# Clearing a gate table in HBM: 20 of its 32 writes issued one stage earlier

## The reference

```
xn = rmsnorm(x);  qa ka va qb kb vb ga gb = split(xn @ w_in)
oa = stick_breaking_attention(qa, ka, va)      # 8 heads
ob = sliding_window_attention(qb, kb, vb)      # 8 q heads, 2 kv heads, window 128, bias, sinks
x  = x + (sigmoid(ga) * (oa @ w_oa) + sigmoid(gb) * (ob @ w_ob)) @ w_o
# product-key experts on t = rmsnorm(x): 8 heads, the best 16 of 128*128 experts each
s, e = top16(scores of t @ wq with the subkeys);  g = softmax(s)
x  = x + sum over heads and choices of  g * gelu(u[e] . t) * v[e]
y  = rmsnorm(x)
```

## Time and profile before

| | us |
|---|---|
| median of three runs | 3921.8 |
| lowest and highest | 3915.57, 3924.2 |
| the profiled execution, its own time | 3913.63 |
| its span in the trace | 3911.9 |
| `route_sample`, first SP instruction to that of `project` | 311.81 to 392.48 |
| `window`, first SP instruction to that of `decide` | 868.26 to 997.75 |

### The profile page before, as it was taken

One profiled execution on the slowest core, in us unless ns is written; L12 is line 12 of the kernel. 1 busy time (PEld: TensorE's weight loads), 2 busy tenths in 40 slices (PEclk: granted clock), 3 DMA queues, 4 the chain that ended last, 5 costly groups with the idle time before them and its releaser, 6 DMA issues. The chain is left out here.

```text
span 3911.9 us, 44636 instructions
## 1 busy us (share of the span) xinstructions
PE 3533.0 (90%) x14123; PEld 2094.6 (54%) x14147; DVE 2613.2 (67%) x5036; ACT 842.1 (22%) x1599; POOL 1655.6 (42%) x1245
## 2 busy tenths in 40 slices
PE   7998799886789999999925999999999999999998
PEld 6445579885466676776722444444444444444443
DVE  0441777755248543545575888888888878888886
ACT  1451211114333345446200000100001000010001
POOL 0000068740123788888772343333333334333331
PEclk8899899997899999999967999999999999999999
DMA  7793389978688775676939999999999999999994
GB/s 267 313 421 145 112 345 395 383 284 300 234 293 284 187 184 108 138 171 115 209 84 397 389 414 400 399 400 373 407 388 394 398 379 404 381 395 406 389 416 179
DMA packets 424235, 1201.13 MB, mean 307 GB/s; under 512 B 150472, under 2 KB 215416, under 8 KB 345336
## 3 DMA queue, kind: packets, MB, share of 16 engines
q0 software_dynamic: 168496, 680.80, 47.0%
q1 hardware_dynamic: 187600, 505.84, 35.0%
q10 hardware_dynamic: 67968, 12.45, 1.8%
HBM read 1127.33 MB, written 72.68 MB: 307 GB/s over the span
## 5 line engine op out<-in xcount | busy, mean ns | idle before, releaser
L2156 POOL DMA_INDIRECT d_ring<-peer_uv,d_idx x512 | 654.3, 1278 | 1081.5 <-DVEq L2210 975.3
L2313 PE MATMUL d_ps<-d_xd,d_u 128*128 128x512 f32 x2048 | 907.4, 596 | 105.6 <-DMA d_u<-u_blocks 87.9
L2324 PE MATMUL d_ps<-d_v,d_a 128*128 128x512 f32 x2048 | 913.6, 600 | 38.8 <-DVE d_a L2216 32.3
L2208 DVE SCALAR_TENSOR_TENSOR d_acc<-d_ring,d_aw,d_acc 128x1024 f32<-128x1024 f32 x512 | 657.7, 1285 | 98.7 <-DVE d_acc L2208 63.6
L2313 PEld LDWEIGHTS d_ps<-d_xd,d_u 128*128 128x128 f32 x2048 | 391.4, 191 | 601.2 <-issue 589.6
L1544 POOL DMA_INDIRECT G<-c_cellg,c_cell x384 | 633.4, 1649 | 142.8 <-issue 120.0
L2324 PEld LDWEIGHTS d_ps<-d_v,d_a 128*128 128x128 f32 x2048 | 393.5, 193 | 540.0 <-issue 539.9
L2196 DVE SCALAR_TENSOR_TENSOR d_ring<-d_ring,d_xn 128x1024 f32<-128x1024 f32 x512 | 605.5, 1220 | 95.3 <-DMA d_qacc<-ys 51.4
L837 POOL DMA_INDIRECT a_x<-peer_uv,a_rowu x128 | 165.9, 1296 | 544.4 <-DVE k_rowv L907 500.9
L2278 ACT ACTIVATE d_ge<-d_h (+1 forms) x256 | 52.1, 203 | 1168.3 <-DVE d_ring L2196 1168.2
L2002 PE MATMUL c_ps<-c_mT,c_chunk 128*128 128x128 f32 x2048 | 239.6, 277 | 8.6 <-DMA c_chunk<-wq 7.5
(11 more groups left out here) (360 smaller groups left out, 4277.7 us busy)
## 6 DMA issues: line engine op xcount, KB each, us to landing
c_chunk<-wq SPq DMA_DIRECT2D x128, 512.0 KB, 4.9
d_u<-u_blocks SPq DMA_DIRECT2D x128, 512.0 KB, 19.1
d_v<-v_blocks SPq DMA_DIRECT2D x128, 512.0 KB, 16.7
s_kc<-sb_kT SPq DMA_DIRECT2D x32, 1024.0 KB, 9.5
s_vc<-sb_v SPq DMA_DIRECT2D x32, 1024.0 KB, 7.4
c_chunk<-w_m SPq DMA_DIRECT2D x64, 512.0 KB, 5.1
d_gb<-G SPq DMA_DIRECT2D x32, 1024.0 KB, 36.0
G<-b_zeros SPq DMA_DIRECT2D x32, 768.0 KB, 8.2
```

What stands on the lines that cost most here:

```text
L2156: pool.indirect_dma_start(out=ring[:, b], out_offset=None, in_=a["peer_uv"], in_offset=bass.IndirectOffsetOnAxis(ap=idx8[par][:, b:b + 1], ...
L2208: nc.vector.scalar_tensor_tensor(acc[T % 2][:], ring[:, b, D:], aw[:, bass.ds(col + n, 1)], acc[T % 2][:], ALU.mult, ALU.add).then_inc(sum ...
L2313: last = nc.tensor.matmul(ps[:, HB + x % 2, :], ub[j][:, k], xd[:, k].rearrange("p t q -> p (t q)"), start=(k == 0), stop=(k == KC - 1))
L2324: last = nc.tensor.matmul(ps[:, VB + c % 4, :], A[u][j][:, q * P:(q + 1) * P], vb[u][j][:, half * 512:half * 512 + 512], start=(j == 0), s ...
```

## The change

Twenty of the 32 writes, rows 0 to 79 of G, are issued in `route_sample`, by SP behind its loads, from a tile of zeros of its own that GpSimd fills; SP waits for them before the block ends. In `window` the eight writes ahead of the loop are gone, and each of its six turns issues two writes instead of four, rows 80 to 127; the wait at the end is for these twelve.

```diff
+CLEARED = 80
 # route_sample
+        zeros = sb("r_zeros", [P, 4, FIRST_HOT * P])
+        zero_done, zero_st = sem("r_zero_done"), sem("r_zero_st")
 # SP, behind the loads of w_r and wq
+                sp.wait_ge(zero_done, 1)
+                for b in range(0, CLEARED, 4):
+                    sp.dma_start(o["G"][b:b + 4, :, 0:FIRST_HOT * P].rearrange("b p t -> p b t"), zeros[:]).then_inc(zero_st, 16)
+                sp.wait_ge(zero_st, 4 * CLEARED)
 # GpSimd
+                nc.gpsimd.memset(zeros[:], 0.0).then_inc(zero_done, 1)
                 for done in spent:
                     pool.sem_clear(done)
 # window, SP
                 sp.wait_ge(zero_done, 1)
-                clear_gates(0, 8)
                 with sp.Fori(0, NP // 2 - 1) as i:
...
                         load_v(t + 1, 1 - u)
-                        clear_gates(32 + 16 * t, 4)
+                        clear_gates(CLEARED + 8 * t, 2)
                 sp.wait_ge(pe_b.sem, pe_b.at(NP - 3, "values"))
                 load_v(NP - 1, 1)
-                sp.wait_ge(zero_st, 16 * P // 4)
+                sp.wait_ge(zero_st, 4 * (P - CLEARED))
```

## The result

The changed kernel takes 3911.55 us in the median of 20 runs, the kernel before 3925.41 on the same chip in 20. The ratio is 0.9963, interval 0.9952 to 0.9974: faster by 14.5 us (10 to 19). The forecast was 23.0 us. Applied to the 3921.8 us from which I predicted, the ratio gives 3907.3, inside my range of 3889 to 3911; the median as measured, 3911.55, lies at its upper edge. In a second set of runs the same kernel gave 0.9943, interval 0.9921 to 0.9964, 22 us (14 to 31). The two intervals overlap between 14 and 19 us.

The account below looks back on a forecast made before the run. No engine bounds the whole span; TensorE's chain bounds the routing stage, and window loads queue behind writes of zeros. Gains of 3.7 and 19.3 us, 23.0 in sum, take the median from 3921.8 to 3898.8 us; range 3889 to 3911.

Parts of the forecast that it names:

- Part 1: Routing stage: twenty writes fit beside TensorE's chain, the last landing near 386 before the stage ends at 392.2; cost zero.
- the 399: Rate in GB/s, read in the window stage from 885 to 895, used to time the twenty writes in the routing stage.
- Part 2: Window stage, ahead of the loop: without the eight writes, scores(2) start at 898.3 for 901.96; gain 3.7 us.
- I take 0.5, near the order of the queue: Window start: the second bias table lands earlier without the writes, so scores(1) start 0.5 us earlier.
- Part 3: Window turns: two writes fewer in each cut two slow gaps from 18.65 to about 9.0 us; gain 19.3 us.
- SP is the later of the two: Window turn: SP's issues, not queued bytes, set when the last k lands, 8.0 to about 9.4 us after V.
- my two terms: Window turn after V: SP issues the last k by 7.4 us; the queue's 2.36 MB take 6.0 us.
- A wait of that size doesn't drop the clock: Window turns: a left-over wait of 0.4 us in each of two gaps leaves TensorE's clock at 1.00.
- Part 4: Window end: still set by the last tile's store, moving from 993.99 to 971; `decide` starts 3.8 us behind as before.
- rival C: Whole kernel: the change does less or nothing to the end, the time returning in a later stage; 3920, 4 in 100.
- Rival B: Window turns: SP's issues and landing, not bytes, keep k 4.1 us late and the clock drops; 3915, 11 in 100.

Follow-up runs that it names:

- e5: All 32 writes issued in the routing stage, none in the window stage, an edit of the changed kernel; ratio to the kernel before 1.0002.
- e10: The kernel before with only the eight writes ahead of the window loop moved to the routing stage, four writes a turn kept, a repeat run; ratio 0.9985.
- e4: The changed kernel with each window turn's two writes issued behind the q and k loads instead of behind v; 3903.3 us, ratio 0.994 to the kernel before.
- e9: The kernel before with each window turn's four writes issued behind the q and k loads, nothing moved to the routing stage; ratio 0.9975.

## Why the prediction was right, and where it was not

*Part 1, the routing stage at no cost: right, within about a microsecond, with most of the slack used up.* Of the 6.5 us that I had between the last landing and the next stage's first load 1.6 were left. Two terms were too small. The rate of a long train of writes was 366 to 382 GB/s; the 399 was read over ten microseconds in which loads ran too. And the sum ended with the last byte at full rate, although writes took 9.4 us and more from issue to landing. e5 shows what is behind the slack: 23 us lost with 12 more writes.

*Part 2, the front writes, 3.7 us: the step failed that takes VectorE's start 0.5 us forward ("I take 0.5, near the order of the queue"), and the clock was left out.* VectorE starts 16.9 us after the stage begins; it was 16.1 before, and I had 15.6. The second bias table lands 9.9 us after its issue, before 9.3. In neither kernel did a write stand ahead of it, and the writes behind had not slowed it.

```profile
885.00 6.47 PE L1254 MATMUL b_ps<-b_k,b_q 64*128 64x128 f32 x32 [12.93 <-DMA b_k<-out_kbT]
899.13 6.48 PE L1254 MATMUL b_ps<-b_k,b_q 64*128 64x128 f32 x32 [7.65 <-DVE b_S L1183]
908.17 6.50 PE L1254 MATMUL b_ps<-b_k,b_q 64*128 64x128 f32 x32 [2.56 <-DVE b_S L1183]
914.60 3.68 PE L1262 MATMUL b_ps<-b_ident,b_W 128*128 128x128 f32 x16
919.40 3.69 PE L1269 MATMUL b_ps<-b_PT,b_v 128*64 128x512 f32 x8 [1.11 <-ACT b_PT L1228]
```

Against the earlier trace rows, scores(2) start at 31.3 us in the stage for 33.7, a gain of 2.4. All traces agree on this: 30.5 to 31.4 us in the six that have both bias loads and no write ahead of the loop, 33.3 to 33.9 in the four with eight writes there, 2.6 apart in the mean. In this trace the last row takes most of it back: the product with v runs at half clock, 3.69 us, where the first trace of before had 1.94. What is left is 0.5 us. But that belongs to the trace and not to the change: the second trace of before has 3.69 there as well, and e10 and e4, without the writes, have 1.94. Over all traces the first tile is stored at 45.4 to 50.2 us with this start, a spread larger than the whole term.

*Part 3, the turns, 19.3 us: the step failed that "SP is the later of the two", with the last k landing 1.8 us after its issue.* In the changed kernel V, the end of values(0), is at about 923.1. SP was quicker than I had it: the last k goes out at 928.2, 5.1 us after V where I had 6.2. But it lands 5.0 us after that, not 1.8, so scores(4) start at 933.32, 10.2 us after V where I had the last k landed at 8.0 to 9.4. The measured 10.2 is neither the later of my two terms (7.4 us of issues, 6.0 of bytes) nor their sum: the two overlap in part. 1.8 was the shortest landing of v. It was too short for k even with no write ahead of it in its turn (3.0 to 3.3 us in e4). What is left of the waits is 1.66 us in the first gap and 0.99 in the second, where I had 0.4. So part 3 gave 13.5 us in the first trace. "A wait of that size doesn't drop the clock" was said of 0.4 us; after the wait of 0.99 in the second gap of the first trace it dropped, 4.3 us of the missing 5.8. In the second trace, after 0.95, it didn't, and the gain of part 3 is 8.6 + 9.2 - 0.9 (a third gap of 9.50) = 16.9, near my 19.3. How many of the timed runs lost the clock there no trace shows. e5 and e4 show the end of it: no left-over and every such gap at 8.6.

*Part 4 and rival C:* right, the gain of the window stage arrives in the time. Single traces show it badly, as other stages spread by up to 15 us (project, 475.8 to 490.8); the window means, 130.6 for before and 113.9 for after, differ by 16.7 us, which is within both measured intervals. Rival B, loads late by SP's issues and not by bytes, was half right: 1.0 to 1.7 us instead of 4.1.

## What to carry to other kernels

A DMA queue is a list in order: before a bulk write is moved to another stage, ask whether it can be issued behind the load that someone waits for. e9 had a window stage as short as the first trace of the changed kernel with one line moved and no write leaving the stage, though its gain in time (3 to 17 us) is less sure; both together (e4) took every wait for k after the start. Take the landing time of a load from a load in the same place of the queue, not from the shortest on record; here it was 5.0 us for 1.8. Count the landing of the last write when a cover is sized. And price a small left-over wait on TensorE with the chance that it costs the clock, and compare stages over more than one trace before a shift in an untouched stage is read as an effect.

## What was not expected of the hardware

The issue of a small load on SP costs more behind writes: q and both k take 1.23 us with no write just ahead, 3.65 behind two writes, and the first pair of k behind two writes 3.47 alone (the changed kernel, at 926.65). A train of 1536-byte runs from SBUF to HBM goes at 366 to 382 GB/s over 24 to 42 us. The same program on the same inputs kept or lost TensorE's full clock (1.00, or 0.70 in the mean of 7 us) at a wait of one microsecond, in two traces; why is open.
